# First norm, projections and both attentions of a hybrid decoder layer as one stage

## The reference, cut to what matters

```python
xn = rmsnorm(x, norm_mix)                    # width 1024
u = xn @ w_in                                # q, k, v (3 x 512), forget gate 8, RWKV 1792, gates 2048
logf = log_sigmoid(fl + b_f)                 # per head and token
# FoX attention, 8 heads of 64; c = cumsum(logf)
s = q @ k.T * 0.125 + c_q[:, None] - c_k[None, :]    # causal
o_a = softmax(s) @ v
# sampled tokens: the same over 16 gathered pages of 128 keys and their own 4 tokens
o_b = rwkv_branch(...)
x += (sig(gA) * (o_a @ p_a) + sig(gB) * (o_b @ p_b)) @ w_o
x += hier_moe(rmsnorm(x, norm_ffn)); y = rmsnorm(x, norm_final)
```

## Time and profile before

| | us |
|---|---|
| median of 3 runs (lowest to highest) | 2316.41 (2313.51 to 2317.73) |
| span of the profiled execution | 2311.8 |
| PE busy in it | 1996.4 (86%) |
| DVE, ACT, POOL busy | 782.8, 394.1, 181.7 |

### The profile page before, as it was taken

The page is one execution under the profiler, slowest core; times in us unless marked ns, Lnnn a source line. Parts: engine busy times, 40 slices in busy tenths (PEclk is TensorE's granted clock), DMA queues, the critical chain, the costliest instruction groups (busy, mean ns, idle before and its releaser), DMA issues. The chain is left out here.

```text
span 2311.8 us, 38704 instructions
## 1 busy us (share of the span) xinstructions
PE 1996.4 (86%) x15421; PEld 1352.3 (58%) x15421; DVE 782.8 (34%) x1567; ACT 394.1 (17%) x835; POOL 181.7 (8%) x358
## 2 busy tenths in 40 slices
PE   4999799967779997999999999789599659999990
PEld 3665477731238786676666666544345347777770
DVE  3000456621203656333333333259613401111115
ACT  4000133300002322111111111111001111111112
POOL 0000144300000000000000000000000231111110
PEclk9999689978899999999999999989699779999995
DMA  3110200069950000110101101172150068888836
GB/s 114 37 37 19 80 5 4 3 235 386 385 190 31 30 35 10 49 39 28 43 30 49 45 30 36 43 264 80 36 210 28 28 217 317 317 315 319 317 130 238
DMA packets 96512, 277.67 MB, mean 120 GB/s; under 512 B 22832, under 2 KB 31536, under 8 KB 86864
## 3 DMA queue, kind: packets, MB, share of 16 engines
q1 hardware_dynamic: 64704, 218.81, 26.3%
q10 hardware_dynamic: 18592, 34.61, 4.2%
q0 software_dynamic: 13072, 22.21, 3.0%
HBM read 244.30 MB, written 39.15 MB: 123 GB/s over the span
## 5 line engine op out<-in xcount | busy, mean ns | idle before, releaser
L1198 PE MATMUL gate_p<-rows,gate_w 128*128 128x352 f32 x768 | 284.1, 489 | 0.0
L952 PE MATMUL rw_pp<-rows,rw_w 128*128 128x264 f32 x896 | 205.8, 391 | 7.7 <-DMA rw_w<-in_w_in 7.7
L952 PEld LDWEIGHTS rw_pp<-rows,rw_w 128*128 128x128 f32 x896 | 171.5, 192 | 40.1 <-DMA rw_w<-in_w_in 7.9
L306 PE MATMUL fox_pp<-rows,fox_w 128*128 128x352 f32 x576 | 172.2, 462 | 4.2 <-DMA fox_w<-in_w_in 4.2
L1198 PEld LDWEIGHTS gate_p<-rows,gate_w 128*128 128x128 f32 x768 | 129.6, 190 | 53.5 <-issue 4.1
L306 PEld LDWEIGHTS fox_pp<-rows,fox_w 128*128 128x128 f32 x576 | 110.1, 191 | 66.1 <-DMA fox_w<-in_w_in 4.6
L1790 PE MATMUL x_p<-late 128*128 128x512 f32 (+1 forms) x288 | 128.5, 601 | 1.5 <-PEq L1513 1.5
L2081 PEld LDWEIGHTS moe_gu<-rows,wgu 128*128 128x128 f32 x1024 | 118.6, 194 | 9.0 <-issue 7.6
L2081 PEld LDWEIGHTS moe_gu<-rows,late 128*128 128x128 f32 x1024 | 116.9, 192 | 8.1 <-issue 8.1
L2081 PE MATMUL moe_gu<-rows,wgu 128*128 128x96 f32 x1024 | 118.4, 277 | 1.1 <-ACT rows L2104 1.1
L2081 PE MATMUL moe_gu<-rows,late 128*128 128x96 f32 x1024 | 116.5, 275 | 0.0
(11 more groups left out here) (357 smaller groups left out, 2906.6 us busy)
## 6 DMA issues: line engine op xcount, KB each, us to landing
wgu<-in_we_gu SPq DMA_DIRECT2D x16, 2048.0 KB, 7.9
late<-in_we_gu SPq DMA_DIRECT2D x16, 2048.0 KB, 8.0
wd<-in_we_down SPq DMA_DIRECT2D x16, 1024.0 KB, 11.8
late<-in_we_down SPq DMA_DIRECT2D x16, 1024.0 KB, 11.8
qkv<-in_cache_kT ACTq DMA_DIRECT2D x48, 256.0 KB, 6.2
qkv<-in_cache_kT SPq DMA_DIRECT2D x48, 256.0 KB, 6.4
qkv<-in_cache_v ACTq DMA_DIRECT2D x48, 256.0 KB, 9.0
qkv<-in_cache_v SPq DMA_DIRECT2D x48, 256.0 KB, 8.8
```

The source lines that it names most:

```text
L306: mm = pe.matmul(pp[j % 2][:, c, 0:N], w[:, j % 2, k, :], e.xnT[:, k, c * N:(c + 1) * N], start=(k == 0), stop=(k == KD - 1))
L952: mm = pe.matmul(pp[u % 2][:, c, 0:QN], w[:, n % 2, k, :], e.xnT[:, k, at:at + QN], start=(k == 0), stop=(k == KD - 1))
L1198: mm = pe.matmul(out[:, 0:GATE_N], gw[:, j % 2, k, :], e.xnT[:, k, at], start=(k == 0), stop=(k == KD - 1))
```

## The change

One stage, `stage_fox`, takes the place of the five.

- x comes transposed (`xT`, made by the host's layout). ACT squares and scales even slices by the gain, DVE adds the squares and scales odd slices. PE projects q tiles 0 and 1 from the unnormalised x and their results are multiplied by the row factor afterwards; xnT is xg times the factor, on DVE. xnT is also stored to DRAM (`xn_d`), since pages are later laid over it.
- v is projected by token (512 columns a matmul), so it isn't turned. The forget gate goes through four 32-column tiles and a summing product.
- The two heads of a pair lie on rows 0 to 63 and 64 to 127; their score products go to PSUM banks of their own. The key gate, broadcast to all rows (`ckb`), is added by DVE in the pass that also takes the extreme; ACT's exp has scale -1. Only the diagonal block gets the mask product. Probabilities are divided by their sum before they are turned; the products with v have v as the stationary side and give o transposed, each head of the pair in its 64 columns. Query tiles go in the order 7, 0, 6, 1, 5, 2, 4, 3.
- The sampled attention is cut into 34 slots (8 key slots, one turning slot, 8 value slots, for each of two groups of four sequences), 8 pages to a slot; one slot is done in each of the 32 units, two behind them. The ring has 28 pages: 12 of their own, 16 over xnT. Even pages are loaded by SP, odd ones by POOL with indirect DMAs; POOL fetches the log gates with indirect DMAs too and widens them to the rows of queries. PE turns them, DVE sums them along the keys.
- `stage_rwkv_front` loads xnT back in four pieces.

The diff, cut to its core:

```diff
--- before.py
+++ after.py
+TILE_ORDER = (7, 0, 6, 1, 5, 2, 4, 3)
+PAGES_KEPT, PAGES_OVER_XN = 12, 16
+RING = PAGES_KEPT + PAGES_OVER_XN
+SLOT = 8
+BG = 4
+CHUNKS = NPG // 2
+SLOTS = [x for _g in range(NB // BG) for x in ([("keys", _g, _n) for _n in range(CHUNKS)] + [("first", _g, 0)]
+                                              + [("values", _g, _n) for _n in range(CHUNKS)])]
...
+            sp.dma_start(w[:, 0], a["w_in"][0]).then_inc(w_loaded[0], 16)
+            for k in range(0, KD, 2):
+                sp.dma_start(xg[:, k], a["xT"][k]).then_inc(x_loaded[k], 16)
+            for j in range(1, 4):
+                sp.dma_start(w[:, j], a["w_in"][j]).then_inc(w_loaded[j], 16)
...
+                if j == 5:
+                    sp.wait_ge(xn_ready, KD)
+                    sp.dma_start(wv, a["w_v"]).then_inc(wv_loaded, 16)
+                    sp.dma_start(e.xn_d, e.xnT).then_inc(spilled, 16)
...
+            def fetch(out, source, column):
+                return pool.indirect_dma_start(out=out, out_offset=None, in_=source,
+                                               in_offset=bass.IndirectOffsetOnAxis(ap=index[:, column:column + 1], axis=0),
+                                               bounds_check=rows - 1, oob_is_err=False)
...
+            def widen(g, c):
+
+                n = g * CHUNKS + c
+                if c == 0:
+                    pool.wait_ge(lf_loaded, 16 * NPG * BG * (g + 1))
+                if n >= 2:
+                    pool.wait_ge(side_made, gate_side(*divmod(n - 2, CHUNKS)) + 1)
+                else:
+                    pool.wait_ge(spread_set, 1)
+                out = lfx[:, n % 2].rearrange("p j (m t) -> p j m t", t=TS)
+                src = lf[:, 2 * c:2 * c + 2, BG * g:BG * g + BG, :].rearrange("p j b h -> p j (b h)")
+                pool.tensor_scalar(out, src.unsqueeze(3).to_broadcast([P, 2, BG * H, TS]), 8.0, None,
+                                   ALU.mult).then_inc(lfx_ready, 1)
+
...
+            project(0, xg, range(KD)).then_inc(made, 1)
+            pe.wait_ge(sq_added, KD)
+            pe.wait_ge(ones_set, 1)
+            for t in range(NTT):
+                mm = pe.matmul(fa[0:size(t), 1, 500 + t:501 + t], acc[:, t * P:t * P + size(t)], e.ones[:, 0:1],
+                               start=True, stop=True)
...
+            for k0 in (0, 4):
+                for c in range(3):
+                    for q in range(4):
+                        mm = pe.matmul(fa[32 * q:32 * q + 32, c, 0:N3], wf[:, k0 + q, :], e.xnT[:, k0 + q, c * N3:(c + 1) * N3],
+                                       start=(k0 == 0), stop=(k0 == 4))
...
+                    mm = pe.matmul((fa[0:n, 3], fb[0:n, 3])[t % 2], e.xnT[:, k, t * P:t * P + n], wv[:, k, :],
                                    start=(k == 0), stop=(k == KD - 1))
...
+                for c in range(0, n, 512):
+                    m = min(512, n - c)
+                    for s in range(2):
+                        pe.matmul(score[s][:, c:c + m], qk[half(s), p, t * P:(t + 1) * P], qk[half(s), HP + p, c:c + m],
+                                  start=True, stop=c + m < n)
+                for s in range(2):
+                    pe.matmul(score[s][:, t * P:n], e.identb[:], e.causalb[:], start=False, stop=True).then_inc(scored, 1)
...
+                for k in range(t + 1):
+                    for s in range(2):
+                        mm = pe.matmul(op[half(s)], v_tok[:, k, (2 * p + s) * DH:(2 * p + s + 1) * DH], probT[:, s, k, :],
+                                       start=(k == 0), stop=(k == t))
+                mm.then_inc(mixed, 1)
...
+                        mm = pe.matmul(dec[32 * b:32 * b + 32, 0:2 * P].rearrange("q (j n) -> q j n", j=2),
+                                       qs[:, g * BG + b, p, :], pair(x * SLOT + 2 * b)[:, :, p * P:(p + 1) * P],
+                                       start=(p == 0), stop=(p == HP - 1))
...
+            for u in range(NU):
+                turn_probs(u, 0)
+                if u + 1 < NU:
+                    scores(u + 1)
+                turn_probs(u, 1)
+                slot(u)
+                mix(u)
+            for x in range(NU, len(SLOTS)):
+                slot(x)
...
+                act.activation(sq[:, k % 2] if k else acc, xg[:, k], ACT.Square).then_inc(squared, 1)
+                if k % 2 == 0:
+                    act.wait_ge(squared, k + 1)
+                    act.activation(xg[:, k], xg[:, k], ACT.Copy, scale=e.v("norm_mix")[:, k:k + 1]).then_inc(xg_even, 1)
...
+                dve.tensor_tensor_reduce(prob[:, u % 2, s, 0:n], score[s][:, 0:n], ckb[:, p % 2, s, 0:n], -0.125, 3.0e38,
+                                         ALU.add, ALU.min, stat[:, u % 2, s, 0:1]).then_inc(biased, 1)
...
+                dve.tensor_tensor_scan(prob_d[:, at], e.ones[:, 0:2 * P], side, prob_d[:, at.start - 1:at.start] if c else 0.0,
+                                       ALU.mult, ALU.subtract).then_inc(side_kept, 1)
...
+            for u in range(NU):
+                keep_high(u, 0)
+                if u + 1 < NU:
+                    bias(u + 1, 0)
+                keep_high(u, 1)
+                if u + 1 < NU:
+                    bias(u + 1, 1)
+                slot(u)
+                if u + 1 < NU:
+                    normalise(u + 1, 0)
+                    normalise(u + 1, 1)
...
+            sp.dma_start(w[:, 0], a["w_in"][8 + ORDER[0]]).then_inc(w_loaded[0], 16)
+            for b in range(4):
+                sp.dma_start(e.xnT[:, 2 * b:2 * b + 2], e.xn_d[:, 2 * b:2 * b + 2]).then_inc(xn_back[b], 16)
+            sp.dma_start(w[:, 1], a["w_in"][8 + ORDER[1]]).then_inc(w_loaded[1], 16)
...
+                    if u == 0 and k % 2 == 0:
+                        pe.wait_ge(xn_back[k // 2], 16)
...
+    a["xT"] = np.ascontiguousarray(a["x"][:NT].T.reshape(KD, P, NT))
```

More of the change, by code:

```diff
@@ L94, in shape_constants @@
     out["own_past"] = np.concatenate([np.where(o, 0.0, NEG) for o in own], 1).astype(np.float32)
[L96 to L103, removed]
+    out["gather8"] = (np.arange(P)[:, None] % NS == np.arange(H)[None, :]).astype(np.float32)
+    out["spread"] = (np.arange(P)[:, None] == np.arange(NS)[None, :] // TS).astype(np.float32)
     out["before"] = (i < j).astype(np.float32)
@@ L240, in _ @@
[L240 to L322, removed]
@@ L366, in _ @@
+            sp.wait_ge(spilled, 16)
+            for i in range(PAGES_KEPT, RING, 2):
+                load_page(i)
             sp.wait_ge(logf_kept, 1)
@@ L371, in _ @@
         @block.tensor
         def _(pe):
[L373 to L384 removed]
+            ident = e.c("ident")
@@ L385, in _ @@
+            for c in range(3):
+                mm = pe.matmul(fa[0:H, c, 0:N3], e.c("gather8"), fs[:, c * N3:(c + 1) * N3], start=True, stop=True)
+            mm.then_inc(z_made, 1)
+            values_of(1)
+            turn_keys(0)
+            values_of(2)
+            turn_keys(1)
+            turn_keys(2)
+            values_of(3)
             pe.wait_ge(logf_ready, 1)
             for t in range(NTT):
-                n = min(P, NT - t * P)
-                mm = pe.transpose(lp[0:n, t, :], e.logfT[:, t * P:t * P + n], e.c("ident")[0:H, 0:H])
@@ L389, in _ @@
-            mm.then_inc(logf_turned, 1)
+                pe.transpose(fa[0:size(t), 0, t * H:(t + 1) * H], logfT[:, t * P:t * P + size(t)], ident[0:H, 0:H])
+            for b in range(NB):
+                q, at = 32 * (b % BG), SEQ + b * TS
+                mm = pe.matmul(fa[q:q + 32, 1, b // BG * TS:(b // BG + 1) * TS], e.c("spread")[0:H, :], logfT[:, at:at + TS],
+                               start=True, stop=True)
+            mm.then_inc(logf_turned, 1)
+            for t in range(4, NTT):
+                values_of(t)
+                turn_keys(t - 1)
@@ new lines, in slot @@
+            def slot(x):
+                kind, g, n = SLOTS[x]
+                if kind == "keys":
+                    keys(g, n)
+                elif kind == "first":
+                    turn_sample(g, 0)
+                else:
+                    values(g, n)
+            scores(0)
+            for u in range(NU):
[5 more added lines that the diff above has]
+                mix(u)
@@ new lines, in _ @@
+            dve.memset(e.eps[:, 0:1], NORM_EPS)
+            dve.memset(e.eps[:, 1:2], GN_EPS)
+            dve.wait_ge(vec_loaded, 16)
+            for k in range(KD):
+                dve.wait_ge(squared, k + 1)
+                if k == 0:
+                    dve.sem_inc(sq_added, 1)
+                else:
+                    dve.wait_ge(sq_added, k)
+                    dve.tensor_tensor(acc, acc, sq[:, k % 2], ALU.add).then_inc(sq_added, 1)
+                if k % 2:
+                    dve.tensor_scalar(xg[:, k], xg[:, k], e.v("norm_mix")[:, k:k + 1], None, ALU.mult).then_inc(xg_odd, 1)
@@ new lines, in values, with slot @@
+            def values(g, n):
+                keep_sample(g, n + 1)
+                if n == CHUNKS - 1:
```

(28 more changed lines are left out.)

1022 lines of the change are left out of this document (531 added, 491 removed).

## The result

| us | before | after | forecast |
|---|---|---|---|
| median (lowest to highest) | 2316.31 (2313.51 to 2317.73) | 2228.32 (2218.18 to 2243.27) | 2071 (2035 to 2150) |
| span of the profiled execution | 2311.8 | 2241.5 | 2066.8 |
| first scores | 267.7 | 340.8 | 201 |
| front's first matmul | 673.9 | 600.8 | 420.7 |

Ratio 0.9624, 95% interval 0.9565 to 0.9684: faster by 88 us, not by 245. The time is outside the range.

A forecast was written before the change was run, and what follows sets the result against it. PE-bound projection and prompt attention stood in a row with DMA-bound sampled stages. Scores at 201, units to 399.6, end 411.6, front 420.7 against 673.9: 253 less, minus 8 for clock, saves 245; 2311.8 - 245 + 4.6 = 2071, range 2035 to 2150.

The forecast's parts named there:

- What must keep up: Sampled page and gate loading: DMA 5.4 us a slot, POOL 5.7 a unit, all below 6.1; no stall counted.
- the 8 us for the clock: PE's clock might drop after the first unit's idle time, costing 0 to 18 us; 8 taken.
- Start: Front of the stage: first slice at 4.5 us, tile 0 done at 23.2, tile 2 begun at 40.6.
- Projections: q and k tiles 2 to 7 86 us, forget gate 3.6, v 61.7, key transposes 4.0; scores at 201.
- First unit: First attention unit, hidden by nothing: scores, biases, exp, reciprocal and product 5.6 us; PE transposes from 206.6.
- Units: 32 units, each two heads of a query tile with a sampled slot: 193 us, ending at 399.6.
- tiles do not run together: Rival for scores and mix: PE's packed tiles run one after another, +50 us, 2121; chance 0.12.
- the 2095: Near half of the separate-tiles rival: each mix pair adds four 64-column weight loads because its heads share all rows.
- Low clock throughout: Rival: PE at 1.2 GHz, a unit 10.5 us, total 2201; chance 0.08.
- Bound by DMA: Rival: VectorE's waits vanish, shape changes are hidden and DMA sets the stage's time, total 2038; chance 0.12.
- POOL late: Rival: POOL's fetches take 2.0 us each, 256 end at 520 us, +108, total 2179; chance 0.05.
- scores later than 215: Sign against the forecast: first attention scores after 215 us, where about 201 was expected.

The follow-up runs named there:

- all plain: The changed kernel with its 128 indirect gate fetches and 128 indirect odd pages made plain DMAs of POOL: 2078.0 us, ratio 0.8960 to the kernel before.
- paced kernel: Against all plain: first 64 gate fetches indirect, each followed by two POOL memsets with a wait for each: 2150.3 us (one execution).
- burst kernel: Against all plain: first 64 gate fetches indirect, back to back: 2080.1 us in one execution, later median 2078.7 and 2076.3 on other chips.

## Why the prediction was wrong

The step that failed is in "What must keep up": "an indirect DMA of 128 rows every 1.29 us ... I count no stall". The 1.30 us held, and so did the queue; 128 gate fetches ended before v's end by plan. I priced the fetches only for POOL, and never asked what they do to another engine: their effect on PE stood in the sum at nothing, without a reason. Rows 8 could not show it: I took from them the spacing and not whether PE ran beside them. What the runs showed in its place is 166 us of loss, in PE's pace and in late news of its results. The span comes apart so: 2241.5 is 174.7 over the 2066.8 forecast.

| term | us |
|---|---|
| gates: scores at 340.8 instead of 209.7 (all plain) | +131.1 |
| start: 209.7 instead of 201 | +8.7 |
| pages: scores to front 260.0 instead of 225.4 (all plain) | +34.6 |
| units and tail: 225.4 instead of 219.7 | +5.7 |
| rest of the kernel 1640.7 instead of 1637.9, and the 8 us for the clock not needed | -5.2 |

By this, 166 of the 175 us are the indirect fetches (131.1 + 34.6); the kernel with all plain ran on another occasion, so a few us either way are open. Point by point, by the kernel with all plain, whose PE in order of time reads:

```profile
122.37 14.36 PE L455 MATMUL fox_b<-rows 128*128 128x352 f32 x48
136.67 3.76 PE L490 MATMUL fox_a<-rows,wf 128*32 128x352 f32 x48
140.35 7.13 PE L501 MATMUL fox_a<-fox_work,rows 128*128 128x512 f32 x16
...
219.44 0.64 PE L610 MATMUL fox_b<-const,lfx 128*128 128x128 f32 x2
220.00 1.93 PE L649 MATMUL fox_b<-pages,qs 128*32 128x256 f32 x32
...
223.19 1.97 PE L590 MATMUL fox_b<-fox_work,v_tok 128*64 128x128 f32 x32 [0.89 <-issue]
225.35 1.77 PE L552 MATMUL fox_a<-qk 64*128 64x512 f32 x8
```

- Start: tile 0 was to be done at 23.2 and ends at 33.9. The first slice landed at 13.5, not 4.5, a number for which I had no row: eight slices and the first weights are on their way at once, and from issue to landing the slices take 10.4 us (ACT's) and 14.0 (SP's) in the median. Tiles 2 to 7 begin at 51.4 for 40.6.
- Projections (their terms add up to 200.4, written as 201): 85.3 us for 86; forget gate 3.8 for 3.6, its column tiles together; a v tile 7.13; the nine with the key transposes and the small products 69.3 (140.35 to 209.67) for 70.2.
- First unit: 6.1 us from the scores to the transposes for 5.6, and the 5.6 was added wrongly: its terms in a row make 6.45.
- Units: from the first scores to the last mix 209.3 us for 198.6, from there to the front 16.1 for 21.1. The tiles do run together: a mix of 8 key tiles is 32 records in 1.97 us (1.7 forecast), their scores 1.77 (1.7). The slot was sized too small: its 16 matmuls take 1.93 by themselves, and I had the two transposes (0.4 to 0.6) within that. What the changes of tile shape cost, forecast at 0.8 us a unit, no run measured by itself. The bias in one pass took 1.222 us over 1024, the 1.225 that I took.
- PE over 0.85: 189.72 of 210 us, 0.90. DMA 0.85 to 1: 0.91. Clock 1.00 soon after 210: 0.98 over the units. All three held, once the fetches were plain.
- Rival "tiles do not run together" (2121) is out, and with it the 2095. The Trainium skill, "TensorE: Matmul & The Clock Gate", section Part 3: Packing small matmuls, would have a weight load wait in the mix, since its heads share their rows; the 1.97 us for 32 records and 32 loads show no such wait, nor did the old projection, whose loads and matmuls all used 128 rows: PE busy 172.18 and its loads 110.13 of 173.5 us. Low clock throughout: out in this form, though a low clock came with the crawl, 0.55 granted from 52 to 205 us. Bound by DMA (2038): near, with 0.91, but not reached.
- "POOL late" had the right engine and the wrong mechanism: POOL kept its 1.30 us, and PE's idle time before its work on pages grew by only 3.6 us. Its wait was seen in the paced kernel alone, at 70 us.
- The tell "scores later than 215 would prove me wrong" fired, at 340.8.

What stays open: what in the chip carries the coupling, and what decides whether it shows. Kernels crawled on the first and the third chip and not on the second and the fourth, but on the first the same instructions crawled at one time and not at another, so the chip alone does not decide it. The chip on which the changed kernel was first timed is not known to be one of these. That PE was fed too slowly with code is not settled: from 52 to 205 us the instruction queues moved one packet where PE crawled and nine where it ran, which does not tell cause from effect. Whether the old kernel is immune was not settled either: its ten executions on the first chip and ten on the fourth ran beside no kernel that crawled. What the pages cost where the gates cost nothing was not tried.

## What to carry to other kernels

Price an operation on every engine that runs beside it, and not only on its own queue: if no row of the trace shows the two together, the bound must include that they disturb each other. Where rows are contiguous in DRAM and the index is one page number, a table entry read into a register and a plain DMA do what a gather does: 150 us less here, in executions where the gather disturbed PE. And before a theory is built or dropped on one execution, run beside it, on the same chip and at the same time, a kernel that shows the effect. Where the profile names a long wait, subtract the time in which the awaited work was not done: only the rest is delay.

## What the runs showed of the hardware that was not expected

- Indirect DMAs of POOL, 1.00 us busy every 1.30 us, went with a PE that started a matmul every 2.8 us instead of every 0.3, and with completions of PE that DVE and ACT saw 11, 52 and 74 us late. Plain DMAs of the same 128 rows (0.54 us busy, 1.2 to 1.3 us apart) did so in no run.
- It depended on the occasion, and perhaps on the chip: the same program took 2144 to 2172 us in four executions on one chip and 2073 to 2082 in eight on two others, and on the first chip the instructions that it shares with the burst kernel crawled from 92 us in one and ran free in the other.
- It set in late and let go: with gates indirect and pages plain PE slowed about 60 fetches after the first, ran at full pace again (35 records in 10 us) for 30 us after a stretch of 5.4 us without an indirect fetch, and slowed again.
- DVE and POOL themselves ran at their usual lengths in the crawl (DVE's 1056-column product 1.26 us); only what PE issued and signalled was late.
